# Gathering the first expert's rows without the last tile's, which TensorE adds from SBUF

## The reference, cut to what matters

```
hn = rmsnorm(h, norm_ffn)
g      = argmax(softmax(hn @ w_rg + b_rg))          # one of 4 groups
gates, expert = top-2 of the 8 experts in group g   # 32 experts in all
# for each expert e, over the tokens that picked it:
y = (silu(x @ w_eg[e]) * (x @ w_eu[e])) @ w_ed[e]
h = h + gate1 * y1 + gate2 * y2
```

## Time and profile before

| | us |
|---|---|
| median of 3 runs | 1089.43 |
| lowest and highest of them | 1088.81, 1089.69 |
| the profiled execution, its own time | 1088.48 |
| the profiled execution, span from first to last instruction | 1086.6 |

### The profile page before, as it was taken

One profiled execution on the slowest core, in us unless ns is written; L12 is line 12 of the kernel. 1 busy time (PEld: TensorE's weight loads), 2 busy tenths in 40 slices (PEclk: granted clock), 3 DMA queues, 4 the chain that ended last, 5 costly groups with the idle time before them and its releaser, 6 DMA issues.

```text
span 1086.6 us, 32851 instructions
## 1 busy us (share of the span) xinstructions
PE 1009.0 (93%) x14634; PEld 820.7 (76%) x14634; DVE 418.0 (38%) x909; ACT 241.7 (22%) x509; POOL 108.1 (10%) x168
## 2 busy tenths in 40 slices
PE   5999999999999999978999999999999999999910
PEld 5786867777686859537888889888888898888810
DVE  1433444535252625362523233232232332323338
ACT  2352222323233322130111111111111011111123
POOL 0110101010101001001111101111011011110000
PEclk9999999999999999998999999999999999999965
DMA  8900000000000000638999999999999999999567
GB/s 262 407 25 40 1 40 0 39 0 39 0 39 0 39 35 5 252 136 322 393 398 400 410 404 402 415 401 410 404 396 410 396 406 396 389 402 389 237 223 298
DMA packets 52930, 262.32 MB, mean 241 GB/s; under 512 B 10285, under 2 KB 12781, under 8 KB 44698
## 3 DMA queue, kind: packets, MB, share of 16 engines
q1 hardware_dynamic: 43130, 234.20, 54.7%
q0 software_dynamic: 7168, 18.10, 4.9%
q10 hardware_dynamic: 2592, 9.44, 2.1%
HBM read 242.00 MB, written 26.80 MB: 247 GB/s over the span
## 4 chain that ended last, share of the span: by engine, by line
PE 89%; DVE 5%; DMA 2%; SPq 2%; issue 1%; ACT 1%; ACTq 0%; DVEq 0%; POOLq 0%
PE bank L1537 32%; PE bank L1257 17%; PE bank L1378 11%; PE bank L1548 10%; PE bank L1309 6%; PE bank L1554 5%; PE bank L1245 4%; SPq L385 1%; DVE arena L1223 1%; DVE arena L1221 1%; DMA arena<-in_w_in 1%; PE bank L1358 1%; DVE arena L1229 1%; PE bank L1316 1%; PE bank L1375 1%
## 5 line engine op out<-in xcount | busy, mean ns | idle before, releaser
L1257 PE MATMUL bank<-xnT,arena 128*128 128x128 f32 x1728 | 201.3, 278 | 4.7 <-DMA arena<-in_w_in 3.2
L1257 PEld LDWEIGHTS bank<-xnT,arena 128*128 128x128 f32 x1728 | 197.1, 194 | 7.4 <-DMA arena<-in_w_in 3.8
L1537 PEld LDWEIGHTS bank<-xnT,arena 128*64 128x64 f32 x4096 | 171.8, 138 | 6.7 <-issue 6.3
L1537 PEld LDWEIGHTS bank<-hnT,arena 128*64 128x64 f32 x4096 | 169.5, 137 | 7.3 <-issue 7.3
L1537 PE MATMUL bank<-xnT,arena 128*64 128x96 f32 x4096 | 175.0, 248 | 0.0
L1537 PE MATMUL bank<-hnT,arena 128*64 128x96 f32 x4096 | 172.7, 247 | 0.6 <-issue 0.6
L1105 DVE TENSOR_SCALAR mixT<-mixT 128x384 f32<-128x384 f32 x32 | 11.6, 363 | 320.8 <-ACT mixT L725 320.8
L1378 PE MATMUL bank<-arena,mixT 128*128 128x512 f32 x256 | 111.7, 594 | 0.0
L1378 PEld LDWEIGHTS bank<-arena,mixT 128*128 128x128 f32 x256 | 48.1, 191 | 57.0 <-issue 57.0
L1548 PE MATMUL bank<-arena,silu_r 128*32 128x384 f32 x768 | 86.2, 488 | 0.5 <-issue 0.5
L1554 PE MATMUL bank<-arena,silu_r 128*32 128x256 f32 x384 | 85.9, 381 | 0.0
(11 more groups left out here) (225 smaller groups left out, 957.4 us busy)
## 6 DMA issues: line engine op xcount, KB each, us to landing
arena<-in_w_eg SPq DMA_DIRECT2D x32, 2048.0 KB, 15.4
arena<-in_w_eu SPq DMA_DIRECT2D x32, 2048.0 KB, 15.6
arena<-in_w_ed SPq DMA_DIRECT2D x32, 2048.0 KB, 16.0
hn_rows<-hs ACTq DMA_DIRECT2D x18, 512.0 KB, 3.0
arena<-pick_rows SPq DMA_DIRECT2D x16, 512.0 KB, 10.4
arena<-in_w_in SPq DMA_DIRECT2D x3, 2048.0 KB, 13.7
arena<-in_w_out SPq DMA_DIRECT2D x1, 4096.0 KB, 23.2
out_y_prompt<-arena SPq DMA_DIRECT2D x8, 512.0 KB, 3.5
```

What stands on the lines that cost most here:

```text
L1257: last = mm(out, w_in_sb[:, k, a:b], xnT[:, k, :], start=k == 0, stop=k == KD - 1)
L1537: last = mm(out[q * SW:(q + 1) * SW, n * BLOCK:(n + 1) * BLOCK], w[:, k, m * P + q * SW:m * P + (q + 1) * SW], rowsT[b][:, k, :], start=k ...
```

## The change

The first expert's rows are fetched in two parts. The rows of its tokens in tiles 0 to 7 are gathered from DRAM with an index column `first_idx` that is copied from `idx_f` as soon as tile 7 has been added; positions that belong to the last tile are still empty and stay zero, since POOL clears `rows[0]` beforehand. The rows of the last tile are in SBUF (`hs`), and TensorE adds them: it multiplies `hs` by `first_sel`, a 128 x 96 matrix with a one where a token of the last tile that picked expert 0 meets its position. The transposes of the gathered rows become multiplications by the identity, so that both parts add up in the same PSUM banks (now 0 and 5). All of this stands between `ranks(8)` and `mark(8)` on TensorE. So that an early gather can be kept to rows of tiles 0 to 7, the row order in `hn_dram` becomes tile by tile: pick k of tile i at (2i + k) * 128. On SP, the up weights of expert 1 now wait for the 18 stores, and the down weights for the gather of expert 1.

```
+EARLY_ROWS = PICK_ROWS - PICKS * P
@@ SP, load_weights(0, 1)
                     sp.wait_ge(s["pe_half_out"], 2)
-                    sp.wait_ge(rows_in[0], 16)
+                    sp.wait_ge(s["hn_stored"], 16 * PICKS * TILES)
                 sp.dma_start(wu[b], ...).then_inc(u_in[b], 16)
+                if isinstance(t, int) and b == 1:
+                    sp.wait_ge(rows_in[1], 16)
                 sp.dma_start(wd[b], ...).then_inc(d_in[b], 16)
@@ POOL
-            pool.wait_ge(s["idx_ready"], 1)
-            pool.wait_ge(s["hn_stored"], 16 * PICKS * TILES)
+            pool.wait_ge(s["u_kept"], 2)
+            pool.wait_ge(s["pooled_ready"], TILES)
+            pool.memset(rows[0], 0.0).then_inc(s["first_rows_zero"], 1)
+            pool.wait_ge(s["first_rows_zero"], 1)
+            pool.wait_ge(s["hn_stored"], 16 * PICKS * (TILES - 1))
+            pool.wait_ge(s["first_idx_ready"], 1)
             gather(0, 0)                  # index first_idx, from hn_dram[0:EARLY_ROWS]
+            pool.wait_ge(s["idx_ready"], 1)
+            pool.wait_ge(s["hn_stored"], 16 * PICKS * TILES)
             gather(0, 1)
@@ DVE, last_rank(j)
                 rank(V.tensor_tensor(M_tok[:, :, :], Mk, token..., ALU.mult))
+                first_of_tile = rt[:, 10:11]
+                rank.then(V.tensor_tensor(first_of_tile, Mk[:, 0, 0:1], Mk[:, 1, 0:1], ALU.add))
                 dve.wait_ge(s["pe_rank"], j + 1)
                 rank.then(V.tensor_tensor(R[:, :], bank[7][:, 64:64 + NE], counts[:, :], ALU.add))
+                V.tensor_scalar(first_sel, con("iota_block"), R[:, 0:1], first_of_tile, ALU.is_equal, ALU.mult).then_inc(s["first_sel_ready"], 1)
@@ DVE, after the loop
             back_idx(j - 1)
+            dve.wait_ge(s["idx_added"], TILES)
+            V.tensor_copy(first_idx[:, :], idx_f[:, 0:1]).then_inc(s["first_idx_ready"], 1)
             back_route(j, last=True)
             last_rank(j)
-            dve.wait_ge(s["idx_added"], TILES)
             dve.wait_ge(s["pe_idx"], TILES)
@@ DVE, rows_turned
+                    got = first_bank[half] if isinstance(e, int) and e == 0 else bank[half]
@@ PE
             ranks(j)
+            pe.wait_ge(s["setup_pool"], 3)
+            pe.wait_ge(rows_in[0], 16)
+            for half in range(2):
+                for k in range(4):
+                    c = (4 * half + k) * P
+                    mm(first_bank[half][:, k * BLOCK:(k + 1) * BLOCK], rows[0][:, c:c + P], ident[0:BLOCK, 0:BLOCK], start=k == 0, stop=False,
+                       skip_group_check=True)
+                if half == 0:
+                    pe.wait_ge(s["hs_ready"], TILES)
+                    pe.wait_ge(s["first_sel_ready"], 1)
+                for k in range(4):
+                    last = mm(first_bank[half][:, k * BLOCK:(k + 1) * BLOCK], hs[:, 4 * half + k, :], first_sel, start=False, stop=True,
+                              skip_group_check=True)
+                if half == 0:
+                    last.then_inc(s["pe_first_rows"], 1)
+            last.then_inc(s["pe_eT"], 1)
             mark(j)
-            pe.wait_ge(s["setup_pool"], 3)
-            turn_rows(0, 0, 16)
             expert(0, 0)
```

More of the change, by code:

```diff
@@ L109, in constants @@
     put("first_e", PER_GROUP - np.arange(PER_GROUP)[None, :])
-    put("pick", p + TILES * P * np.arange(PICKS)[None, :] - NO_ROW)
+    put("pick", p + P * np.arange(PICKS)[None, :] - NO_ROW)
     put("valid", (p < SAMPLE) | (p >= SAMPLE + PADS))
@@ L294, in build @@
         rowsT = [xnT[:, :, 0:BLOCK], hnT[:, :, 0:BLOCK]]
+        first_bank = (bank[0], bank[5])
+        first_sel = gate_work[:, 0, 0, 0:BLOCK]
         sig = mixT[:, 0:3, :].rearrange("p k n -> p (k n)")
@@ L300, in build @@
         assert NH <= 3 * P
+        first_idx = sb("first_idx", [BLOCK, 1], I32)
         rows_idx = [sb(f"rows_idx{b}", [BLOCK, 1], I32) for b in range(2)]
@@ L319, in build @@
             pe_xT pe_z pe_gate pe_qk pe_u pe_r pe_v pe_pool pe_kT pe_scores pe_kv pe_o pe_ones pe_wout pe_hT
-            pe_router pe_rank pe_idx pe_half_out pe_own_T pe_first_rows pe_hist_T pe_small_T
+            pe_router pe_rank pe_idx first_idx_ready first_sel_ready first_rows_zero pe_half_out pe_own_T pe_first_rows pe_hist_T pe_small_T
             setup_dve setup_pool w_up_zero z_ready qk_ready ge_ready eb_ready enb_ready edec_ready u_ready er_ready v_ready kz_ready
@@ L444, in _ @@
                 for k, y in ((0, y1[i]), (1, y2[i])):
-                    at_row = (k * TILES + i) * P
+                    at_row = (PICKS * i + k) * P
                     sp.dma_start(y[0:OUT_ROWS[i], :], y_dram[at_row:at_row + OUT_ROWS[i], :]).then_inc(y_in[i], 16)
@@ L479, in _ @@
                 windows(i)
-            pool.wait_ge(s["idx_ready"], 1)
-            pool.wait_ge(s["hn_stored"], 16 * PICKS * TILES)
             def gather(t, b):
                 e = 2 * t + b
-                if isinstance(t, int):
+                rows_of = hn_dram
+                if isinstance(t, int) and e == 0:
+                    index = first_idx[:, :]
+                    rows_of = hn_dram[0:EARLY_ROWS, :]
+                elif isinstance(t, int):
                     index = idx_i[:, e:e + 1]
@@ L492, in gather @@
                     wait_parted(pool, s["row_idx_ready"], e - 3, s["parted"])
-                nc.gpsimd.indirect_dma_start(rows[b], None, hn_dram, bass.IndirectOffsetOnAxis(ap=index, axis=0),
-                                             bounds_check=PICK_ROWS - 1, oob_is_err=False).then_inc(rows_in[b], 16)
+                nc.gpsimd.indirect_dma_start(rows[b], None, rows_of, bass.IndirectOffsetOnAxis(ap=index, axis=0),
+                                             bounds_check=(EARLY_ROWS if isinstance(t, int) and e == 0 else PICK_ROWS) - 1, oob_is_err=False).then_inc(rows_in[b], 16)
             def scatter(t, b, first=False):
@@ L635, in back_h @@
                 for k in range(PICKS):
-                    act.dma_start(hn_dram[bass.ds(k * TILES * P + j * P, P), :], hs[:, :, :].rearrange("p k n -> p (k n)")).then_inc(s["hn_stored"], 16)
+                    act.dma_start(hn_dram[bass.ds(j * (PICKS * P) + k * P, P), :], hs[:, :, :].rearrange("p k n -> p (k n)")).then_inc(s["hn_stored"], 16)
             def back_o(j, steps=back):
@@ L714, in _ @@
             for k in range(PICKS):
-                at_row = k * TILES * P + j * P
+                at_row = (PICKS * j + k) * P
                 act.dma_start(hn_dram[at_row:at_row + P, :], hs[:, :, :].rearrange("p k n -> p (k n)")).then_inc(s["hn_stored"], 16)
@@ L1009, in back_idx @@
                 dve.wait_ge(s["pe_idx"], j + 1)
-                rank(V.tensor_scalar(token[:, :], token[:, :], float(P), None, ALU.add))
+                rank(V.tensor_scalar(token[:, :], token[:, :], float(PICKS * P), None, ALU.add))
                 V.tensor_tensor(idx_f[:, :], idx_f[:, :], bank[7][0:BLOCK, 192:192 + NE], ALU.add).then_inc(s["idx_added"], 1)
@@ L1097, in rows_turned @@
                     k = slice(half * KD // 2, (half + 1) * KD // 2)
-                    V.tensor_tensor(rowsT[b][:, k, :], bank[half][:, 0:4 * BLOCK].rearrange("p (k n) -> p k n", n=BLOCK),
+                    got = first_bank[half] if isinstance(e, int) and e == 0 else bank[half]
+                    V.tensor_tensor(rowsT[b][:, k, :], got[:, 0:4 * BLOCK].rearrange("p (k n) -> p k n", n=BLOCK),
                                     g_ffn[:, k].unsqueeze(2).to_broadcast([P, KD // 2, BLOCK]), ALU.mult).then_inc(s["eT_ready"], 1)
@@ L1187, in _ @@
                         table(PICKS * i + k, k)
-                    V.tensor_scalar(token[:, :], token[:, :], float(P), None, ALU.add).then_inc(s["x_dve"], 1)
+                    V.tensor_scalar(token[:, :], token[:, :], float(PICKS * P), None, ALU.add).then_inc(s["x_dve"], 1)
                     dve.wait_ge(s["x_dve"], i + 1)
@@ L1525, in turn_rows @@
                         last = turn(bank[half][:, k * BLOCK:(k + 1) * BLOCK], rows[b][:, c:c + P], BLOCK)
-                    if isinstance(e, int) and e == 0 and half == 0:
-                        last.then_inc(s["pe_first_rows"], 1)
                 last.then_inc(s["pe_eT"], 1)
```

## The result

| | median us (lowest to highest, runs) |
|---|---|
| before | 1088.91 (1087.78 to 1095.02, 22) |
| after | 1091.65 (1089.52 to 1093.61, 22) |
| ratio after to before | 1.0023, 95% interval 1.0017 to 1.0030 |

The change made the kernel slower by 0.23%, 2.5 us (1.9 to 3.3). Forecast were 1.1 us less and a range up to 1091.0. The profiled execution of after took 1092.32 us, its span is 1090.5.

A forecast was written before the change was run, and what follows sets the result against it. TensorE alone was taken to bound the kernel from 495 us. Landing 487.4, multiplications 4.9 low and 1.0 full, `mark` 0.45, DVE 2.7, `up` 10.71 gave 507.1 against 508.2, 1.1 us less: 1088.3 us, range 1086.1 to 1091.0.

The forecast's parts named there:

- The early gather: First expert's gather on POOL: starts at 482.15 and lands at 487.4, bounds 486.4 to 488.9.
- the unhindered 486.4: Lower bound for the first gather's landing, with no contention from the last tile's stores.
- A record of the new multiplications: Each of 32 TensorE records before `mark(8)` takes 0.21 us at the low clock, 0.11 at full.
- The factor of 4 for transposes: Rival for the 16 multiplications: each costs 4x a transpose, 7.0 us at full clock; 2.5 us more, 1091.9; chance 0.03.
- The clock: TensorE's clock falls near 486, rises 4.9 us into the multiplications and holds, so `up` takes 10.71 instead of 12.81 us.
- the clock rises at 492.3: During the new multiplications, 4.9 us after 487.4; 23 records done by then, nine more at full clock.
- What waits behind `mark(8)`: DVE's `idx_i`, gates and pooling copies (2.07 us) plus scaling (0.61) lie exposed before the first `up`: 2.7 us.
- The gap and the clock: PE's 2.7 us pause between `mark(8)` and `up`, shorter than the earlier 3.5, leaves the clock at full level.
- the clock falls in the new gap: Rival: the 2.7 us pause after `mark(8)` lowers the clock, `up` loses 2.8; 1.7 us more, 1091.1; chance 0.13.
- The sum: From gather landing to the end of the first `up`: 507.1 against 508.2, 1.1 us less.
- What comes after needs no further look: From 495 us TensorE alone sets the time; moving the first `up` moves the end equally, if no weight or gather is late.
- The remark that landings take 16 us in the steady state: Expert 1's down weights, 16.0 us from issue, land at 515.5 against a need at 525: slack 9 us.

The follow-up runs named there:

- e13: Changed kernel with the 16 multiplications done twice over, 64 records of 96 columns; one run, 1098.06 us.
- e1: Changed kernel with `mark(8)` moved ahead of the 16 multiplications; median 1090.12 us, 1.0003 of the kernel before.
- e2: Changed kernel with DVE's scaling of the first expert's rows moved ahead of `idx_i`, gates and pooling copies; median 1089.20 us, 0.9999 of the kernel before.
- e3: Changed kernel with the multiplications streaming 128 columns instead of 96; 1.0009 of the kernel before.
- e14: Changed kernel with the multiplications 128 columns wide and done twice over, 64 records; one run, 1091.42 us.
- e6: Changed kernel with `mark(8)` ahead of the multiplications, 96 columns, and 20 idle-time multiplications into an unread bank; median 1089.04 us, 1.0009 of the kernel before.
- e8: Changed kernel with eight transposes replacing all 16 multiplications, the last tile's rows of the first expert left out; median 1086.97 us, 0.9993 of the kernel before.
- the light versions of the first two: e6 and e7 with only the first half of each expert's down weights loaded; 1084.96 and 1086.57 us, 0.9962 and 0.9981 of the kernel before.
- e7: Kernel before with idle-time multiplications: 14 before `ranks(8)`, 6 before `mark(8)`, 22 during the gather; median 1092.44 us, 1.0039 of the kernel before.
- the light pair: Kernel before and changed kernel, each with only the first half of each expert's down weights loaded; 1088.68 and 1090.08 us.
- e5: Changed kernel with `mark(8)` ahead of the multiplications and 128 columns streamed; median 1087.89 us, 0.9990 of the kernel before.
- e16: The same kernel as e5, run again; median 1087.83 us, 0.9986 of the kernel before.
- e11: e6 with only the first half of each expert's down weights loaded; 1084.96 us, 0.9962 of the kernel before.
- e4: Changed kernel with 96 columns of router weights in place of the identity and `first_sel`; 1.0021 of the kernel before.

## Why the prediction was wrong, point by point

- **The early gather: right.** 0.93 us from its index to its start was forecast, 1.02 came; it landed at 489.1, which is 487.2 on the clock of the profile before, forecast 487.4. That is 0.8 us later than the unhindered 486.4, nearly all of it a longer transfer (4.95 us against 4.22). It ran beside the stores, as the forecast assumed; no run separates the two.
- **A record of the new multiplications: right.** 0.214 us low and 0.11 full against 0.21 and 0.11. The factor of 4 for transposes, which the Trainium skill gives in "TensorE: Matmul & The Clock Gate", Terms, did not appear: a product took two records of 0.214 us where a transpose took one of 0.19.
- **The clock: wrong, and this is the step that failed.** The forecast put "the clock rises at 492.3" from two rows of restarts, one of which was streaming 128 columns and the other mostly `up`, with more than twice as many records in a microsecond. It took any back-to-back work to be as good. In none of the seven profiles with 96 columns under a 128-column weight load in which the clock had fallen did it rise before the first `up`, not even in 13.9 us (e13). So all 32 records were low (7.1 us instead of 5.9), `mark(8)` ran low (0.55 instead of 0.45), and its end came 1.2 us later than forecast (495.0 on the clock of before, forecast 493.75). `up`, expected at 10.71, took 12.53.
- **What waits behind `mark(8)`: right.** Forecast 2.7 us, came 2.55; e1 and e2 remove it from either side. It is a loss in its own right. With it gone the changed kernel only equals the one before (ratios 1.0003 and 0.9999), though its bridge is 1.3 and 1.1 us shorter.
- **The gap and the clock: the assumption that it holds was not safe either.** The forecast argued that 2.7 us are shorter than 3.5. In e3 the clock rose and fell again 2.8 us after the end of `mark(8)`. In e14 the same gap did not bring it down. So the rival "the clock falls in the new gap" came true in one of two profiles in which there was something to lower; in the changed kernel the clock was low already. Its number, 1091.1, is near what came, but by another way, so that is luck.
- **The sum:** 1.1 us less was forecast, the bridge came out 1.8 us longer: 1.2 from the late `mark(8)`, 1.8 from `up`, 0.1 less from the gap.
- **"What comes after needs no further look": right for this kernel, wrong as a rule.** No wait for weights appears in either profile of after, so most of its loss is the bridge's. Yet e6 to e8 and the light versions of the first two show that a gain of 3 to 5 us would have arrived in a part of the executions only, and in e7 in none. The remark that landings take 16 us in the steady state looked at slack and not at the share of 1.02.
- **Left open:** the bridge explains 1.8 of the 2.5 us (interval 1.9 to 3.3), and the light pair differs by 1.4. The two profiles of after hold little of the rest: from the end of the first `up` to the last `down` they need 529.7 and 530.0 us against 529.6 before. Whether it is weight stream in executions that were not profiled wasn't measured. Profiles of one kernel start up to 1.9 us apart before the first tile is done, which is more than what is missing. Why the same stream moves 393 GB/s when it is behind and 402 when it isn't, and what sets the start of the waits at 867 us, stays open as well. So does the cause of the "issue" waits.

## What to carry to other kernels

When work is moved in front of an instruction, look at what else hangs on that instruction: here an index table, gates and two copies that had been free as long as a DMA covered them. A pause filled with multiplications need not bring the granted clock back, whatever TensorE's busy share says: look for a clock row of that very shape before its rise is put into a sum. And before pricing an earlier start, look at the second busiest resource of the long stretch behind it; with the DMA engines at a share of 1.02, microseconds gained ahead of it were in the median mostly not delivered.

## What the runs showed of the hardware that was not expected

- fp32 multiplications of 96 columns with 128-column weights, back to back with PE at a busy share of 1.00, left the granted clock at 0.50 for 13.9 us (e13); with 128 columns at the same seven records a microsecond it rose after 3.7, 5.2, 5.2 and 6.6 us (e14, e5, e16, e3). `up`, with 96 columns behind 64 of weights and sixteen records a microsecond, had it rise 1.5 to 5.4 us after its start (e1, e8). Records of the narrow kind did not bring a full clock down: in e6 and e11 all 32 ran at 1.00. Dense or nearly empty operands made no difference (e4 against after).
- Keeping TensorE busy ahead of the new multiplications paid in the bridge: with 20 multiplications in idle time (e6) the 16 new ones took 3.6 us and the first `up` 10.8, where the same kernel without them (e1) needed 6.9 and 11.4. Yet that was worth nothing in the median time while the DMA share stood at 1.02 (1.0009 of before, interval 0.9995 to 1.0023).
- In the profiled executions of e7 and e8 the waits for weights began at 867 us and came back in one expert after the other, 12 and 15 times in all, with loads that took 28.8 us to land (e7; before at most 24.0 for weights) and a slightly lower rate (393 and 392 against 402 GB/s).
